# Ten slabs before and ten slabs after the mixer's output projection: seven products of 128x128 blocks for eight, with the sums of weight blocks on GpSimd

## The reference, cut to what matters

```python
def mixer_ab(h, w_in, v_g, s_w, s_b, w_out):
    z = h @ w_in                              # 256 x 1024 by 1024 x 2560
    u, v, g_a, x_b, g_b = jnp.split(z, ...)
    v = layer_norm(v, v_g)...
    sv = einsum(v, s_w) + s_b
    y_a = u * sv * silu(g_a)
    f = real(fft2(x_b))
    y_b = f * silu(g_b)
    return concatenate([y_a, y_b]) @ w_out
...
    q, k, v, g = split_c(h @ w_in)            # 256 x 1024 by 1024 x 2560
    q = rope_2d(q), k = rope_2d(k)
    o = window_attention(q, k, v, k_c, v_c, sink)
    y = (o * silu(g)) @ w_out_c
```

## Time and profile before

| what | value |
|---|---|
| three runs | 1088.62, 1086.25, 1089.25 us; median 1088.62 us |
| profiled execution, first to last instruction | 1085.9 us |
| PE busy | 1049.5 us, 97% |
| DVE, ACT, POOL busy | 393.8, 286.9, 54.1 us |
| HBM read | 333.02 MB |

### The profile page before, as it was taken

The page is one execution under the profiler, slowest core; times in us unless marked ns, Lnnn a source line. Parts: engine busy times, 40 slices in busy tenths (PEclk is TensorE's granted clock), DMA queues, the critical chain, the costliest instruction groups (busy, mean ns, idle before and its releaser), DMA issues.

```text
span 1085.9 us, 15938 instructions
## 1 busy us (share of the span) xinstructions
PE 1049.5 (97%) x6296; PEld 723.5 (67%) x6296; DVE 393.8 (36%) x1026; ACT 286.9 (26%) x658; POOL 54.1 (5%) x87
## 2 busy tenths in 40 slices
PE   6999999999998999999899999999989999999998
PEld 4787786688745655665356655665458888887577
DVE  1298977533632232112112122222332021523851
ACT  3124136611521121212111121113223111213951
POOL 0000202013100000000000000001000001100001
PEclk9999999999999999999999999999999999999999
DMA  9999387965699999999999999999998334310001
GB/s 386 340 420 421 164 347 307 421 253 200 248 374 422 405 420 419 421 421 420 421 421 421 409 421 422 420 422 421 420 416 336 116 120 155 114 39 1 1 2 39
DMA packets 49611, 335.12 MB, mean 309 GB/s; under 512 B 5472, under 2 KB 7872, under 8 KB 9984
## 3 DMA queue, kind: packets, MB, share of 16 engines
q1 hardware_dynamic: 46976, 329.01, 74.5%
q10 hardware_dynamic: 2176, 3.37, 1.0%
q0 software_dynamic: 384, 1.70, 0.4%
HBM read 333.02 MB, written 1.05 MB: 308 GB/s over the span
## 4 chain that ended last, share of the span: by engine, by line
PE 89%; DMA 5%; DVE 4%; issue 1%; ACT 1%; SPq 0%; DVEq 0%; ACTq 0%
PE bank L1199 14%; PE bank L574 10%; PE bank L1242 7%; PE bank L1154 5%; PE bank L1351 5%; DMA ring<-experts 5%; PE bank L1020 4%; PE bank L1044 3%; PE bank L1087 3%; PE bank L493 3%; PE bank L904 3%; PE bank L1394 3%; PE bank L920 3%; PE bank L1450 2%; PE bank L707 2%; PE bank L640 2%
## 5 line engine op out<-in xcount | busy, mean ns | idle before, releaser
L1199 PE MATMUL bank<-ring,arena 128*32 128x512 f32 (+1 forms) x1112 | 176.8, 605 | 9.4 <-DMA ring<-experts 9.4
L1199 PEld LDWEIGHTS bank<-ring,arena 128*32 128x32 f32 (+1 forms) x1112 | 52.4, 121 | 113.8 <-issue 113.7
L574 PE MATMUL bank<-hT,ring 128*128 128x256 f32 x512 | 113.0, 381 | 0.7 <-ACT hT L1656 0.7
L574 PEld LDWEIGHTS bank<-hT,ring 128*128 128x128 f32 x512 | 96.5, 190 | 18.1 <-issue 5.4
L1242 PE MATMUL bank<-ring,conds 128*32 128x512 f32 (+1 forms) x560 | 87.8, 596 | 6.2 <-DMA ring<-experts 3.5
L2511 DVE TENSOR_TENSOR yhalf<-bank,yhalf 128x512 fp32r<-128x512 f32 x48 | 33.2, 692 | 80.3 <-ACT yhalf L1866 80.3
L1825 ACT ACTIVATE arena<-bank,mod 128x256 f32<-128x256 f32 x96 | 40.3, 472 | 77.5 <-PE bank L1020 77.3
L1242 PEld LDWEIGHTS bank<-ring,conds 128*32 128x32 f32 (+1 forms) x560 | 27.1, 119 | 49.0 <-issue 43.3
L1590 POOL TENSOR_TENSOR hT<-hT 128x256 f32<-128x256 f32 x30 | 21.8, 726 | 740.4 <-ACT hT L1650 739.0
L1020 PE MATMUL bank<-picked,halves 128*128 128x256 f32 x384 | 57.2, 292 | 0.4 <-ACT arena L1825 0.4
L1351 PE MATMUL bank<-hT,ring 128*128 128x256 f32 x256 | 57.0, 379 | 0.0
(11 more groups left out here) (427 smaller groups left out, 1504.5 us busy)
## 6 DMA issues: line engine op xcount, KB each, us to landing
ring<-experts SPq DMA_DIRECT2D x187, 1024.0 KB, 13.4
ring<-stream SPq DMA_DIRECT2D x118, 1024.0 KB, 11.9
ring<-experts SPq DMA_DIRECT2D x8, 512.0 KB, 9.5
resid<-x SPq DMA_DIRECT2D x1, 1024.0 KB, 5.0
resid<-ctx ACTq DMA_DIRECT2D x1, 1024.0 KB, 10.1
keys_room<-experts SPq DMA_DIRECT2D x1, 1024.0 KB, 6.9
arena<-stream SPq DMA_DIRECT2D x1, 1024.0 KB, 7.9
hT<-stream SPq DMA_DIRECT2D x1, 1024.0 KB, 7.6
```

Source lines behind the costliest of these rows:

```text
L574: mm = mmul(o[:, 0:n_tok], w[:, k, t * P:(t + 1) * P], hT[:, k, 0:n_tok], start=(k == 0), stop=(k == KT - 1))
L1199: mm = mmul(o[at:at + n_slots, :], xg_of(m, kk)[:, at:at + n_slots], w[g][:, k, :], start=(kk == 0), stop=(kk == KT - 1))
```

## The change

Each of the twenty slabs is taken as a product of 2 x 2 blocks: the weights are cut into `a11, a12, a21, a22` (tiles k 0 to 3 or 4 to 7, columns 0 to 127 or 128 to 255), the tokens into `b11, b12, b21, b22` (k 0 to 3 or 4 to 7, tokens 0 to 127 or 128 to 255). Seven products with sums of blocks take the place of eight. Each product is four matmuls of 128x128 by 128 columns.

- PE (`seven`, `product_by_seven`, `first_two`): parts 1, 5, 7, 6 go to four quarters of one bank ("F"), parts 2, 4, 3 to three quarters of a second one ("L"); three banks (2, 3, 4) are used in turn. The first two slabs of a stage are interleaved.
- POOL (`add_quarters`): four sums of weight blocks per slab, each `tensor_tensor` of 128 x 512, both operands in SBUF. Slabs 0 and 1 come after `sq4c`, slabs 2 to 13 after the wait for `sq3` and the load of `cs_late`, slabs 14 to 19 after `partial_sums("sq4")`. The sums have four rooms (`weight_sums`): `pT`, the context half of the residual, one room of the ring, which is taken out of it (`held_rooms`), and `pr`. A room is free when slab i-4 is multiplied.
- DVE (`scaled_and_added`): four sums of token blocks per stage, each 128 x 512 from SBUF, between the scales of `h3` and `h4`; per slab three additions on the F bank (`midway`: 128, 256 and 128 columns, one operand in PSUM, one in SBUF) and one of 384 or two of 256 and 128 on the L bank (`ending`). The rotations go by slab: a shuffle and three `tensor_tensor` of 512 columns for five slabs, where there were ten tiles with 256 columns each.
- ACT: one copy of 128 columns per slab (`keep_first`) and for eight of the slabs a Silu of 512 columns in SBUF (`through_silu`), in place of two reads of 256 columns from PSUM.
- Order: in stage 1 the u slabs (6, 7) come last; in stage 2 two q slabs and `v2` 0 and 1 come last. The scores of heads 0 to 3 stand before and after slab `("cin", 4)`. Some semaphores are merged (`constants_set`, `late`).

```diff
+FAST = [("ab", s) for s in (0, 1, 2, 3, 4, 5, 8, 9, 6, 7)] + [("cin", s) for s in (0, 2, 3, 6, 7, 8, 9, 4, 5, 1)]
...
+            held_rooms.append(given[0].pop(6))
...
+            def seven(i, part):
+                b11, b12, b21, b22 = token_quarters()
+                a11, a12, a21, a22 = weight_quarters(i)
+                sums, turned_sums = weight_sums(i), token_sums(i)
...
+                def product(name, at, a, b, ready=0):
+                    o = bk(name)
+                    for k in range(4):
+                        if ready:
+                            h_tile(tag, ready - 1 + k)
+                        lhs, rhs = (b, a) if by_tokens(i) else (a, b)
+                        mm = mmul(o[:, at:at + P], lhs[:, k, :], rhs[:, k, :], start=k == 0, stop=k == 3)
+                    return mm
+                if part == 1:
+                    open_group(first, first_bank(i))
+                    product(first, 0, a11, b11, ready=1 if i % 10 == 0 else 0)
+                elif part == 5:
+                    pe.wait_ge(S("token_sums"), 4 * stage + 1)
+                    wait_sums(pe, i, 1)
+                    product(first, third_at(i), sums[:, 0, :, :], turned_sums[:, 0, :, :])
...
+                elif part == 2:
+                    open_group(second, second_bank(i))
+                    product(second, 0, a12, b21, ready=5 if i % 10 == 0 else 0)
...
+            def product_by_seven(i):
+                take_fast(i)
+                for part in (1, 5, 7, 6, 2, 4, 3):
+                    seven(i, part)
+            def first_two(i):
+                take_fast(i)
+                take_fast(i + 1)
+                for n, part in ((0, 1), (1, 1), (0, 5), (1, 5), (0, 2), (0, 7), (0, 6), (0, 4), (0, 3), (1, 7), (1, 6), (1, 2), (1, 4), (1, 3)):
+                    seven(i + n, part)
...
-            for i in range(16):
...
+            first_two(0)
+            product_by_seven(2)
+            product_by_seven(3)
+            over_channels(0)
+            product_by_seven(4)
...
+            over_chunk(2)
+            over_chunk(3)
+            product_by_seven(9)
...
+            def add_quarters(i):
+                room_free(pool, i)
+                pool.wait_ge(slab_in[slot_of[fast_slab[i]]], 16 * loads[fast_slab[i]])
+                a11, a12, a21, a22 = weight_quarters(i)
+                to = weight_sums(i)
+                made = 4 * i
+                g.tensor_tensor(to[:, 0, :, :], a21, a22, ALU.add).then_inc(S("sums_by_pool"), 1)
+                g.tensor_tensor(to[:, 2, :, :], a11, a21, ALU.subtract).then_inc(S("sums_by_pool"), 1)
+                pool.wait_ge(S("sums_by_pool"), made + 1)
+                g.tensor_tensor(to[:, 1, :, :], to[:, 0, :, :], a11, ALU.subtract).then_inc(S("sums_by_pool"), 1)
+                pool.wait_ge(S("sums_by_pool"), made + 3)
+                g.tensor_tensor(to[:, 3, :, :], a12, to[:, 1, :, :], ALU.subtract).then_inc(S("sums_by_pool"), 1)
+
             partial_sums("sq4c", side=1)
+            add_quarters(0)
+            add_quarters(1)
             pool.wait_ge(S("sq3"), 1)
             pool.dma_start(cs_late, consts2_d[:, DFT_W:C2_W]).then_inc(S("late_in"), 16)
+            for i in range(2, 14):
+                add_quarters(i)
             partial_sums("sq4")
-            full(pool, ("k2", 1))
+            for i in range(14, 20):
+                add_quarters(i)
+            full(pool, ("v2", 3))
...
+            def scaled_and_added(i):
+                for k in range(5):
+                    scale(tag, k)
+                dve.wait_ge(S(tag), 4)
+                v.tensor_tensor(to[:, 0, :, :], b12, b11, ALU.subtract).then_inc(S("token_sums"), 1)
+                for k in range(5, KT):
+                    scale(tag, k)
+                dve.wait_ge(S(tag), KT)
+                v.tensor_tensor(to[:, 2, :, :], b22, b12, ALU.subtract).then_inc(S("token_sums"), 1)
...
+            def midway(i):
+                dve.wait_ge(S("first_kept"), i + 1)
+                o, to = bk(("F", i)), kept[:, i % 2, :]
+                link(v.tensor_tensor(common, o[:, 3 * P:4 * P], to[:, 0:P], ALU.add))
...
+            def ending(i):
+                full(dve, ("L", i))
+                for at, to in fast_out(i)[0]:
+                    n = to.shape[1]
+                    last = v.tensor_tensor(to, bk(("L", i))[:, at:at + n], kept[:, i % 2, at:at + n], ALU.add)
+                emptied(last, ("L", i))
```

More of the change, by code:

```diff
@@ new lines, in has_silu, with all_of, wait_sums @@
+        def has_silu(i):
+            return FAST[i] in [("ab", s) for s in (4, 5, 8, 9)] + [("cin", s) for s in (6, 7, 8, 9)]
+        SILU_NUMBER = {i: n + 1 for n, i in enumerate(j for j in range(len(FAST)) if has_silu(j))}
+        def all_of(eng, src):
+            i = FAST.index(src)
+            done(eng, ("L", i))
+            if has_silu(i):
+                eng.wait_ge(S("silu_rest"), SILU_NUMBER[i])
+        def wait_sums(eng, i, n):
+            eng.wait_ge(S("sums_by_pool"), 4 * i + n)
@@ L352, in build, with room_free @@
+        def room_free(eng, i):
+            if i >= 4:
+                full(eng, ("L", i - 4))
+            elif i == 0:
+                full(eng, ("oabc", KT - 1))
+            elif i == 1:
+                eng.wait_ge(S("h4c"), KT)
+            elif i == 2:
+                full(eng, ("gu", LAST))
+            else:
+                for b in range(4):
+                    done(eng, ("sums", b))
         slab_in = [S(f"slab_in{k}") for k in range(RING)]
@@ L685, in last_attention @@
                     if i == 1:
-                        for t in range(4):
+                        done(pe, ("L", FAST.index(("cin", 1))))
+                        for t in range(2, 4):
                             done(pe, ("v2", t))
@@ L1642, in root @@
             def root(n, src, tag, cols, parts=P):
[L1644 to L1645 removed]
+                which = "late" if tag in LATE else tag
+                act.wait_ge(S(which + "_ms"), LATE.get(tag, n))
+                a.activation(src[0:parts, 0:cols], src[0:parts, 0:cols], ACT.Sqrt).then_inc(S(which + "_rt"), 1)
             root(1, rstd, "n1", 256)
@@ L1910, in _, with keep_first, through_silu, channels_out @@
                 emptied(a.copy(k2[:, t, T:2 * T], bk(("k2c", t))[:, 0:T]), ("k2c", t))
[L1911 to L1914, removed]
-            root(1, bn[:, 0:2, 13], "v", 2)
[L1916 to L1928, removed]
+            def keep_first(i):
+                full(act, ("F", i))
+                a.copy(kept[:, i % 2, 0:P], bk(("F", i))[:, 0:P]).then_inc(S("first_kept"), 1)
+            def through_silu(i):
+                done(act, ("L", i))
+                at = fast_out(i)[2]
+                a.activation(at, at, ACT.Silu).then_inc(S("silu_rest"), 1)
+            def channels_out(n):
+                full(act, ("fa", n))
+                if n >= 2:
+                    full(act, ("fb", n - 2))
+                emptied(a.copy(fa[:, n % 2, :], bk(("fa", n))[:, 0:T]), ("fa", n))
+            for i in range(3):
+                keep_first(i)
+            root(1, bn[:, 0:2, 13], "v", 2)
+            load_table(ACT.Silu)
+            keep_first(3)
+            keep_first(4)
+            channels_out(0)
+            channels_out(1)
+            keep_first(5)
+            through_silu(4)
+            channels_out(2)
+            keep_first(6)
+            through_silu(5)
+            channels_out(3)
+            keep_first(7)
+            through_silu(6)
+            keep_first(8)
+            through_silu(7)
+            keep_first(9)
             load_table(ACT.Sqrt)
@@ L1943, in _ @@
             v2_tile(3)
[L1944 to L1957, removed]
+            for i in range(10, 18):
+                keep_first(i)
+                if has_silu(i - 1):
+                    through_silu(i - 1)
+                if i == 17:
+                    exponents("c", 0)
+            keep_first(18)
             exponents("c", 1)
-            v2_tile(1)
+            keep_first(19)
             for i in range(8):
@@ L2681, in c_out, with whole @@
                 full(dve, ("c", "o", i))
-                done(dve, (f"g2{i // 2}", i % 2))
+                all_of(dve, ("cin", 6 + i // 2))
                 emptied(v.tensor_tensor(o2[:, i, :], bk(("c", "o", i))[:, 0:256], g2s[:, i, :], ALU.mult), ("c", "o", i))
-            for h in range(4):
-                c_scores(h)
+            def whole(i):
+                midway(i)
+                ending(i)
+            whole(10)
+            rotate(10)
+            whole(11)
+            rotate(11)
+            whole(12)
+            rotate(12)
+            whole(13)
+            whole(14)
+            whole(15)
+            whole(16)
+            c_scores(0)
+            c_scores(1)
+            whole(17)
+            rotate(17)
+            c_scores(2)
+            c_scores(3)
+            whole(18)
+            rotate(18)
+            midway(19)
             for i in range(8):
```

251 lines of the change are left out of this document (177 added, 74 removed).

## The result

The changed kernel takes 1089.87 us (median of 15 runs, 1087.79 to 1092.56), the kernel before 1088.61 us beside it (15 runs, 1086.25 to 1089.25). The ratio is 1.0016, 95% interval 1.0009 to 1.0024: by the 0.3% of the prediction no change, and if anything a shade slower. The forecast was 1082.9 us. The time lies inside the range, but the gain of 5.7 us is not there. The profiled execution of the changed kernel has a span of 1088.4 us, 2.5 us more than before.

What follows compares the result with a forecast made beforehand. PE's pace was taken to bound both stages. -13.4 + 5.8 + 0.3 + 0.55 + 1.0 = -5.75 us, so 1088.6 becomes 1082.9 us, range 1075 to 1091.

Steps and rivals of the forecast that it cites:

- What the change takes from PE: All twenty slabs: seven narrow products at 6.23 us replace 6.90 us, winning 0.67 us a slab, 13.4 us in all.
- rival C: The narrow matmul pace does not last, weight loads come one after the other: 1165 us, or about 1128; chance 0.03.
- Start of stage 1: POOL's sums for slabs 2 and 3 hold DVE's h3 scales and token sums, so PE waits: loss 5.8 us.
- The first two scales get by: Start of stage 1: two h3 scales pass unheld, end 814.9; each later one takes 1.36 us, hold 0.95 included.
- End of stage 1: PE's oabx wants y_a 3 at 3.0 us after slab 9, held products make it 3.3: loss 0.3 us.
- Start of stage 2: Part 1 takes a tile in 0.22 us while tiles come at 0.41: loss 0.55 us.
- In stage 2: Rotations held by POOL's sums, 7.4 us a slab against PE's 6.23, mostly absorbed by PSUM banks: loss 1.0 us.
- POOL's sum: A POOL sum of 512 columns takes 1.20 us, 4.9 us a slab, so POOL is never late by pace.
- B: Holds last the whole POOL sum and eat the gain at stage 1's start, rotations, norm and gates: 1092 us; chance 0.22.
- Rival A: POOL and DVE miss each other, only 0.55 us are lost: 1075.7 us; chance 0.2.

Runs made afterwards that it cites:

- e3_both: The changed kernel, with POOL resting until the h3 token sums are made and ACT copying k2c tile 0 ahead of the shifts: 1075.34 us, ratio 0.9885.
- e2_bank: The changed kernel, with ACT copying the first tile of k2c out of its bank ahead of the eight h3 shifts: 1082.81 us, ratio 0.9949.
- e1_rest: The changed kernel, with POOL waiting after the sums of slabs 0 and 1 until DVE has made the four h3 token sums: 1079.87 us, ratio 0.9915.
- e4_rest_one: The changed kernel, with POOL resting for the h3 token sums only ahead of slab 3, after slab 2's sums: 1085.61 us, ratio 0.9972.
- e7_linked_sums: The kernel before, plus 16 unused POOL sums of 512 columns behind the cs_late load, each waiting for the one before it: 1098.28 us, ratio 1.0092.

## Why the prediction was wrong, point by point

- *What the change takes from PE* was right: -13.4 us forecast. Stage 2 gave 6.1 us net, and stage 1 without its lost start (e3_both) 5.7 us net; with the 0.5 us at the start of stage 2 and the 0.7 us before `oabx` put back, that is 13.0. Waits that are met cost nothing, the product takes 0.893 us over the whole stage, and rival C is ruled out. (Its 8.9 us for a slab should be 9.0, 1.45 times 6.23; that changes nothing.)
- *Start of stage 1: 5.8 us.* **This is the step that failed.** It measured 12.8 us (25.32 less 12.50), of which 10.0 lie ahead of the second product, in the wait for the bank and what came before it, and 2.8 in slow products behind it. Three things were missing or wrong in it:
  - The bank. The prediction let part 1 of slab 1 wait for `hT` alone; it also opens a bank that holds `k2c`, and ACT empties that behind its eight shifts. Delaying the scales delays the shifts and so the copy. With the copy moved ahead (e2_bank) the start loses 8.0 us and not 12.8, and the kernel is 0.5% faster than before, 5.6 us by the ratio, against 5.7 forecast. That this is so near is in part luck: 8.0 us is not 5.8, and the 1.0 us of stage 2 did not come.
  - The clock. The prediction held that waits under 3.3 us each leave it up, from the earlier trace rows. In e1_rest a single wait of 2.03 us was followed by a granted clock of 0.50 from 819.45 to 822.86, and a product of 1.71 us in place of 0.89. In the change it was 0.50 from 820.52 to 834.17. Of the 4.9 us that the table has beside the waits, 2.8 are the products behind 828.52; the other 2.1 are in the first product, whose four matmuls ran one by one and, but for the first, at the lower clock; they lie ahead of 828.52, where the bank decides. No run has the same waits at the full clock, so the clock's share is read from rows and not tested by itself.
  - "The first two scales get by": none did. The first was held for 3.2 us and not 0.95. In e2_bank and e4_rest_one it got by, and the second was held for 3.9 us. The later pitch was well taken, 1.41 us against 1.36. The waits for tiles that come of the holds alone were 4.2 us (4.5 in e2_bank), below the 5.8 forecast, which was reckoned for token sums that bind; the bank and the clock hid that.
- *End of stage 1: 0.3 us.* 0.7, the same in every kernel with the change; the profile names no engine for it, so that it is the wait for `y_a` is not shown.
- *Start of stage 2: 0.55 us.* The first 16 matmul records take 0.54 us longer than two products. Right.
- *In stage 2: 1.0 us.* Nothing. The rotations are held (sums of 512 columns take up to 1.76 us in place of 0.69), and PE is busy throughout; none of it reached PE.
- *POOL's sum: 1.20 us.* 1.22 from start to start, and 1.34 behind a link.
- Left over: in the profiled execution of the change PE comes to stage 1 1.56 us later than before. Over the kernels here that moment lies between 815.0 and 818.1 us, and PE's waits for the experts' loads sum to 14.0 us in this execution against 12.9 in that of the kernel before, so I count it as scatter; no run tested it.

On the profiled spans: +1.6 - 13.0 + 12.8 + 0.7 + 0.5 + 0.1 (output projection) - 0.2 (attention) = +2.5 us, the difference of 1088.4 and 1085.9.

Of the rivals, B came nearest in time (1092), but not in its reasons: neither a hold of 1.25 us nor late rotations made the loss. What it named as an addition, the lower clock while PE is half idle, did come. Rival A's time of 1075.7 us, that of POOL and DVE missing each other, is what e3_both brought about by hand: 1075.34.

## What to carry to other kernels

When an instruction becomes late, list all that stands behind it on its own queue and on the queue of whoever waits for it, with the PSUM banks that those would free: here it was the copy of another tile behind eight shifts. Moving that copy alone won 4.9 us of the 12.8, keeping POOL off the scales alone 8.9, both together all of it. Where two engines hold each other up, let the one with slack rest while the other prepares the next stage; one wait on POOL and one copy moved up turned no gain into 1.15%. Price a wait on PE with the slow matmuls that may follow it: in e1_rest the wait was 2.0 us and the loss 3.9.

## What the hardware did that I had not expected

- A DVE instruction with two SBUF operands can stand behind a whole row of POOL instructions that read SBUF, not just the one under way: `gs` for 18.3 us behind sums with no pause and 7.8 us behind copies. With a link behind every sum (1.35 to 1.41 us from start to start) it got in at once.
- A pause is not the only way in. In the change `gs` at 810.49 took 0.39 us and was through (810.88) about when the next sum began (810.81), with no link between the two; and once the scales had begun to alternate with sums, they went on at 1.41 us across sums without a link. What decides between standing back and taking turns is open.
- To begin first did not help. In e2_bank the second scale's row begins at 813.80, POOL's next sum at 814.12, and the scale was held over that sum and two more. In e4_rest_one it went the same way (4.32 us from 815.78, the sum at 816.10).
- In a turn, DVE is held for 1.0 us (1.41 less 0.41) of a sum that takes 1.22 alone, and fills hold nothing.
- PE's granted clock fell to 0.50 after a wait of 2.03 us in e1_rest, and in e7_linked_sums with no wait above 0.71 us, in a stretch where PE got one tile per 1.4 us. In e3_both, where PE never waited there, it stayed at 1.00.
